# The first gather of a mixture of experts: its index from one comparison with the ranks of expert 0, and each token's 16 gates carried behind its row

## The reference

```python
g_logits = xt @ w_rg + b_rg                       # 4 groups
g_idx, g_p = argmax(g_logits), its softmax value
e_sel = (xt @ w_re + b_re)[group g_idx]           # the 4 experts of that group
top_v, top_i = top_k(e_sel, 2)
top_w = softmax(top_v) * g_p
gate[token, e] = top_w for the two chosen experts, 0 for the other 14
for e in range(16):
    h = silu(xt @ w_gate[e]) * (xt @ w_up[e])     # 1024 -> 512
    y += gate[:, e] * (h @ w_down[e])             # 512 -> 1024
x = layer_norm(alpha * x1 + y)
```

## Time and profile before

| | us |
|---|---|
| three runs | 896.71, 896.92, 899.1 |
| median | 896.92 |
| the profiled execution | 895.64 |
| its span | 894.0 |

### The profile page before, as it was taken

One profiled execution on the slowest core, in us unless ns is written; L12 is line 12 of the kernel. 1 busy time (PEld: TensorE's weight loads), 2 busy tenths in 40 slices (PEclk: granted clock), 3 DMA queues, 4 the chain that ended last, 5 costly groups with the idle time before them and its releaser, 6 DMA issues.

```text
span 894.0 us, 12720 instructions
## 1 busy us (share of the span) xinstructions
PE 820.6 (92%) x4267; PEld 713.6 (80%) x4268; DVE 590.3 (66%) x741; ACT 442.5 (50%) x495; POOL 272.6 (30%) x261
## 2 busy tenths in 40 slices
PE   6999999999999999279999999999999999999910
PEld 6999999998788886268888888888888888888810
DVE  4099999956676554889998983148911533947184
ACT  5211232546633223438888893258822734846252
POOL 1423564562000000034343432124312321433263
PEclk9999999999999999579999999999999999999965
DMA  8211111103647331569999999149962572983453
GB/s 291 55 48 47 47 47 48 47 1 114 242 176 271 118 124 48 154 231 313 392 392 370 394 394 324 29 101 364 390 218 63 160 229 46 350 306 65 110 241 139
DMA packets 59550, 167.57 MB, mean 187 GB/s; under 512 B 6841, under 2 KB 25274, under 8 KB 55430
## 3 DMA queue, kind: packets, MB, share of 16 engines
q1 hardware_dynamic: 51318, 144.57, 43.6%
q0 software_dynamic: 8208, 22.70, 11.6%
HBM read 144.79 MB, written 28.76 MB: 194 GB/s over the span
## 4 chain that ended last, share of the span: by engine, by line
PE 89%; DVE 6%; DMA 1%; issue 1%; ACT 1%; POOL 0%; POOLq 0%; SPq 0%; ACTq 0%; DVEq 0%
PE PS L1627 32%; PE PS L1378 19%; PE PS L1644 16%; PE PS L1557 10%; PE PS L1356 6%; PE PS L1528 2%; DVE C L1125 1%; PE PS L1405 1%; PE PS L1445 1%; PE PS L1509 1%; DVE RAW L1298 1%; DVE BIG L399 1%; DMA F<-in_x_prompt 1%; DMA F<-x_rows,MIX 0%; PE PS L1468 0%
## 5 line engine op out<-in xcount | busy, mean ns | idle before, releaser
L1627 PE MATMUL PS<-BIG,TH 128*128 128x512 f32 x1248 | 295.9, 393 | 1.5 <-DVE TH L1281 1.5
L1627 PEld LDWEIGHTS PS<-BIG,TH 128*128 128x128 f32 x1248 | 233.6, 189 | 49.4 <-issue 1.9
L1378 PE MATMUL PS<-BIG,WD 128*128 128x352 f32 x1080 | 177.4, 325 | 0.0
L1378 PEld LDWEIGHTS PS<-BIG,WD 128*128 128x128 f32 x1080 | 174.9, 188 | 0.9
L340 DVE TENSOR_TENSOR BIG<-RAW,BIG 128x2048 fp32r<-128x2048 f32 x64 | 145.1, 2288 | 24.1 <-ACT BIG L943 24.1
L1644 PE MATMUL PS<-WD,TH 128*128 128x512 f32 x624 | 155.8, 399 | 0.0
L1644 PEld LDWEIGHTS PS<-WD,TH 128*128 128x128 f32 x624 | 113.6, 189 | 22.1
L943 ACT ACTIVATE BIG<-RAW 128x2048 fp32r<-128x2048 f32 x64 | 119.3, 1908 | 15.6 <-PE PS L1557 7.9
L293 DVE SCALAR_TENSOR_TENSOR PS<-RAW,C,PS 128x512 f32<-128x512 f32 x174 | 115.4, 746 | 0.0
L1557 PE MATMUL PS<-BIG,WD 128*128 128x512 f32 (+1 forms) x432 | 100.7, 392 | 1.8 <-DVE BIG L399 1.8
L1557 PEld LDWEIGHTS PS<-BIG,WD 128*128 128x128 f32 (+1 forms) x432 | 76.7, 179 | 22.7 <-issue 1.3
(11 more groups left out here) (217 smaller groups left out, 770.1 us busy)
## 6 DMA issues: line engine op xcount, KB each, us to landing
RAW<-in_w_gate SPq DMA_DIRECT2D x64, 512.0 KB, 7.5
RAW<-in_w_up SPq DMA_DIRECT2D x64, 512.0 KB, 9.0
MIX<-in_w_down SPq DMA_DIRECT2D x32, 1024.0 KB, 10.5
F<-in_w_in SPq DMA_DIRECT2D x17, 512.0 KB, 4.1
F<-in_x_prompt SPq DMA_DIRECT2D x10, 512.0 KB, 4.8
x_rows<-F SPq DMA_DIRECT2D x9, 512.0 KB, 2.7
sum_rows<-F SPq DMA_DIRECT2D x9, 512.0 KB, 3.6
RAW<-in_w_out SPq DMA_DIRECT2D x4, 1024.0 KB, 6.1
```

The source lines that it names most:

```text
L1378: mm = pe.matmul(bank(3 * q + g, GRP), win[:, q, ws, c, :], xT[:, xs_, c, g * GRP:(g + 1) * GRP], start=(c == 0 and ws + xs_ == 0), stop=( ...
L1627: mm = pe.matmul(bank(h), xe[:, xs_, c, :], w, start=(c == 0 and xs_ + ws == 0), stop=(c == KD - 1 and xs_ == 1))
```

## The change

*A first index of its own.* VectorE compares, for the nine tiles of tokens, the rank in expert 0 (with 1,024 taken off for its members, `FAR`) with the numbers -1024 to -897. The result `ohf` is a one-hot of the place within the first tile, for the first 128 members of expert 0. Nine matmuls of two columns sum two parts of the token's number into bank 5, and `idxc` is made from them. The first gather waits for this, for the stored rows and for the stored gates, and no longer for the table.

*Gates behind the rows.* The gate weights are worked out ahead of the ranks, spread over 16 columns (`gate_rows`) and stored by SP into 16 new columns of `x1_dram`, whose rows are now 1,040 long. Each gather brings them along; GpSimd copies them (`keep_gates`) into 16 columns of `gates` for each tile, and `y_copy` takes the column of tile and expert. The one-hots `otw`, their eighteen matmuls and the sums behind them are gone.

*Order.* On TensorE the transposes of the first tile now stand ahead of the table's matmuls. On VectorE `xe_lo` of the first tile stands ahead of the table, and `lo_unit` 1 to 5 all behind the table.

```diff
-    x1_dram = nc.dram_tensor("x1_rows", (TOK + P, D), F32).ap()
+    x1_dram = nc.dram_tensor("x1_rows", (TOK + P, D + NE), F32).ap()
...
+        ohf = mx(NT * P // 2).bitcast(BF16).rearrange("p (i m) -> p i m", i=NT)
+        igf, key0, pm = mx(P), mx(NT), mx(1)
+        vc0 = mx(NT).bitcast(BF16).rearrange("p (i w) -> p i w", w=2)
+        firstf = mx(2)
...
+        gate_rows, gate_part = (mx(NT * NE).rearrange("p (i e) -> p i e", i=NT) for _ in range(2))
+        gates = mx(NE * NTAB)
...
+        xg_gated = F2[:, 0:D + NE]
...
                 for u in range(6):
                     wait_lo(sp, e - 1, u)
                     load_unit(sp, e, u)
+                    if u == 0 and isinstance(e, int):
+                        sp.wait_ge(S("gates_spread"), 1)
+                        sp.dma_start(x1_dram[0:SEQ, D:].rearrange("(i p) e -> p i e", p=P), gate_rows[:, 0:NT - 1, :]
+                                     ).then_inc(S("gates_stored"), 16)
+                        sp.dma_start(x1_dram[SEQ:TOK, D:], gate_rows[0:NS, NT - 1, :]).then_inc(S("gates_stored"), 16)
...
             def gather(t):
-                pool.wait_ge(S("index_copied"), t + 1)
+                pool.wait_ge(S("index_copied"), t)
+                pool.wait_ge(S("gates_in"), t)
                 pool.tensor_tensor(carrier[:, 0:1], epsc, epsc, ALU.add)
-                pool.indirect_dma_start(xg, None, x1_dram, bass.IndirectOffsetOnAxis(ap=idxc, axis=0),
+                gather_rows()
+
+            def gather_rows():
+                pool.indirect_dma_start(xg_gated, None, x1_dram, bass.IndirectOffsetOnAxis(ap=idxc, axis=0),
                                         bounds_check=TOK - 1, oob_is_err=False
                                         ).then_inc(S("rows_in"), 16)
 
+            def keep_gates(t):
+                pool.tensor_copy(gates[:, ds(t * NE, NE)], xg_gated[:, D:]).then_inc(S("gates_in"), 1)
+
+            pool.wait_ge(S("x1_stored"), 16 * NT)
+            pool.wait_ge(S("gates_stored"), 32)
+            pool.wait_ge(S("first_index"), 1)
+            gather_rows()
+            pool.wait_ge(S("rows_in"), 16)
+            keep_gates(0)
             pool.wait_ge(S("table_ready"), 1)
-            index(0)
-            pool.wait_ge(S("x1_stored"), 16 * NT)
-            gather(0)
-            pool.wait_ge(S("rows_in"), 16)
             index(1)
             pool.wait_ge(S("xe_turned"), 1)
             gather(1)
             pool.wait_ge(S("rows_in"), 32)
+            keep_gates(1)
             index(2)
...
-                act.wait_ge(S("gates_ready"), 1)
+                act.wait_ge(S("gates_in"), t + 1)
                 act.activation(yrow, PS[:, 5:7, :].rearrange("p b n -> p (b n)"), ACT.Copy,
-                               scale=gates[:, ds(t, 1)]).then_inc(S("y_copied"), 1)
...
-            dve.wait_ge(S("route_consts"), 6)
+            dve.wait_ge(S("route_consts"), 8)
+            dve.tensor_copy(vc0[:, :, 0], tokid[:, 0:NT]).then_inc(S("first_values"), 1)
...
+            dve.wait_ge(S("exps"), 2)
+            do(dve.tensor_reduce(gsum, ge, AX, ALU.add))
+            do(dve.reciprocal(gp, gsum))
+            do(dve.tensor_scalar(rs, ex, ALPHA, ALPHA, ALU.mult, ALU.add))
+            do(dve.reciprocal(rs, rs))
+            do(dve.tensor_tensor(wgt[:, 0], rs, gp, ALU.mult))
+            do(dve.tensor_tensor(wgt[:, 1], wgt[:, 0], ex, ALU.mult))
+            for k, out in enumerate((gate_rows, gate_part)):
+                do(dve.tensor_tensor(out, flat[k], over(wgt[:, k], NE), ALU.mult))
+            dve.tensor_tensor(gate_rows, gate_rows, gate_part, ALU.add).then_inc(S("gates_spread"), 1)
+
             dve.wait_ge(S("ranked"), 1)
+            rk = bank(7, NT * NE).rearrange("p (i e) -> p i e", i=NT)
+            do(dve.scalar_tensor_tensor(key0, Mb[:, :, 0], -float(FAR), rk[:, :, 0], ALU.mult, ALU.add))
+            dve.tensor_scalar(vc0[:, :, 1], key0, -1.0, pm, ALU.mult, ALU.add).then_inc(S("first_values"), 1)
+            dve.wait_ge(S("x1_ready"), NT)
+            dve.tensor_tensor(ohf, igf.rearrange("p (i m) -> p i m", i=1).to_broadcast((P, NT, P)),
+                              key0.rearrange("p (i m) -> p i m", m=1).to_broadcast((P, NT, P)), ALU.is_equal
+                              ).then_inc(S("first_hot"), 1)
             counts_ps = bank(7)[:, NT * NE:(NT + 1) * NE]
...
+            dve.wait_ge(S("first_sum"), 1)
+            do(dve.tensor_copy(firstf, bank(5, 2)))
+            dve.scalar_tensor_tensor(idxc, firstf[:, 0:1], padc, firstf[:, 1:2], ALU.add, ALU.add
+                                     ).then_inc(S("first_index"), 1)
...
-            dve.wait_ge(S("exps"), 2)
-            do(dve.tensor_reduce(gsum, ge, AX, ALU.add))
-            do(dve.reciprocal(gp, gsum))
-            do(dve.tensor_scalar(rs, ex, ALPHA, ALPHA, ALU.mult, ALU.add))
-            do(dve.reciprocal(rs, rs))
-            do(dve.tensor_tensor(wgt[:, 0], rs, gp, ALU.mult))
-            do(dve.tensor_tensor(wgt[:, 1], wgt[:, 0], ex, ALU.mult))
-            dve.wait_ge(S("table_sum"), 1)
-            do(dve.tensor_copy(tabf, bank(6, 2 * NTAB)))
-            dve.scalar_tensor_tensor(table, tabf[:, 0:NTAB], padc, tabf[:, NTAB:], ALU.add, ALU.add
-                                     ).then_inc(S("table_ready"), 1)
-
-            part = [wpart[0][:, 0], wpart[0][:, 1], wpart[1][:, 0]]
-            do(dve.tensor_copy(part[0], wgt))
-            do(dve.tensor_tensor(wrem[0], wgt, part[0], ALU.subtract))
-            do(dve.tensor_copy(part[1], wrem[0]))
-            do(dve.tensor_tensor(part[2], wrem[0], part[1], ALU.subtract))
-            for h in range(3):
-                dve.tensor_tensor(otw[:, :, :, h, :], ohe,
-                                  part[h].rearrange("p k (i m) -> p k i m", m=1).to_broadcast(four), ALU.mult
-                                  ).then_inc(S("gate_hot"), 1)
-
-            lo_unit(dve, 0, 1)
-            lo_unit(dve, 0, 2)
...
-            dve.wait_ge(S("gate_sum"), 1)
-            do(dve.tensor_copy(gatep, bank(7, 3 * NTAB)))
-            do(dve.tensor_tensor(gates, gatep[:, 2 * NTAB:], gatep[:, NTAB:2 * NTAB], ALU.add))
-            dve.tensor_tensor(gates, gates, gatep[:, 0:NTAB], ALU.add).then_inc(S("gates_ready"), 1)
+            dve.wait_ge(S("table_sum"), 1)
+            do(dve.tensor_copy(tabf, bank(6, 2 * NTAB)))
+            dve.scalar_tensor_tensor(table, tabf[:, 0:NTAB], padc, tabf[:, NTAB:], ALU.add, ALU.add
+                                     ).then_inc(S("table_ready"), 1)
             do(dve.tensor_scalar(tabf[:, 0:NTAB], tabf[:, 0:NTAB], padc, None, ALU.add))
             do(dve.tensor_tensor(tabf[:, 0:NTAB], tabf[:, 0:NTAB], tabf[:, NTAB:], ALU.add))
             do(dve.tensor_scalar(tabf[:, NTAB:], tabf[:, 0:NTAB], float(SEQ), 4096.0, ALU.is_lt, ALU.mult))
             dve.scalar_tensor_tensor(table_s, tabf[:, 0:NTAB], -float(SEQ), tabf[:, NTAB:], ALU.add, ALU.add
                                      ).then_inc(S("sample_table"), 1)
-            for u in (3, 4, 5):
+            for u in range(1, 6):
                 lo_unit(dve, 0, u)
...
+            pe.wait_ge(S("first_values"), 2)
+            pe.wait_ge(S("first_hot"), 1)
+            for i in range(NT):
+                M = rows_of(i)
+                mm = pe.matmul(bank(5, 2), ohf[0:M, i], vc0[0:M, i], start=(i == 0), stop=(i == NT - 1))
+            mm.then_inc(S("first_sum"), 1)
...
+            pe.wait_ge(S("rows_in"), 16)
+            for c in range(KD):
+                mm = turn(bank(2 + c // 4)[:, (c % 4) * P:(c % 4 + 1) * P], xg[:, c:D:KD], P)
+                if c == KD // 2 - 1:
+                    mm.then_inc(S("half_turned"), 1)
+            mm.then_inc(S("xe_turned"), 1)
             for c in range(2):
                 pe.wait_ge(S("one_hot"), c + 1)
                 for i in range(NT):
                     mm = pe.matmul(bank(6, 2 * NTAB), ohp[0:M, c, i], oht[0:M, c, i].rearrange("p h m -> p (h m)"),
                                    start=(c + i == 0), stop=(c == 1 and i == NT - 1))
             mm.then_inc(S("table_sum"), 1)
...
-            for c in range(2):
-                for i in range(NT):
-                    M = rows_of(i)
-                    if c + i == 0:
-                        pe.wait_ge(S("gate_hot"), 3)
-                    mm = pe.matmul(bank(7, 3 * NTAB), ohp[0:M, c, i], otw[0:M, c, i].rearrange("p h m -> p (h m)"),
-                                   start=(c + i == 0), stop=(c == 1 and i == NT - 1))
-            mm.then_inc(S("gate_sum"), 1)
-            pe.wait_ge(S("rows_in"), 16)
-            for c in range(KD):
-                mm = turn(bank(2 + c // 4)[:, (c % 4) * P:(c % 4 + 1) * P], xg[:, c:D:KD], P)
-                if c == KD // 2 - 1:
-                    mm.then_inc(S("half_turned"), 1)
-            mm.then_inc(S("xe_turned"), 1)
```

More of the change, by code:

```diff
@@ L50 @@
 EPS = 1e-5
+FAR = 1024
 ALPHA = 2.0 ** 0.25
@@ L727, in tile @@
                 pool.wait_ge(S("rows_in"), 16 * t + 48)
+                keep_gates(t + 2)
```

(7 more changed lines are left out.)

32 lines of the change are left out of this document (10 added, 22 removed).

## The result

| | before | changed |
|---|---|---|
| median us | 896.60 | 898.73 |
| lowest and highest of 12 | 895.58, 899.10 | 897.52, 901.36 |
| profiled execution, span | 895.64, 894.0 | 900.63, 899.0 |

The ratio is 1.0024, 95% interval 1.0014 to 1.0034: the changed kernel is 2.1 us slower, where 2.5 us faster was forecast. The time lies above the range.

What follows compares the result with a forecast made beforehand. Routing before the first tile was taken as the limit, TensorE being never idle afterwards. The tile starts 4.9 us sooner, subtractions take back 2.4: −2.5, profiled 893.1, median 894.4 us; range 892.9 to 898.0.

Steps and rivals of the forecast that it cites:

- What bounds the kernel: Expert stage: TensorE never idle, tiles repeat every 17.79 us, so a gain counts only if the first tile ends earlier.
- Routing and first index: Routing on VectorE and TensorE: gates spread at 370.2, the first gather's index ready at 373.6.
- The gate store: SP's store before the first gather: issued at 370.2, landing 1.0 behind a load of 374.4, at 375.4; bounds 373.6 and 377.4.
- late-store rival: Gate stores before the first gather land late: loss after 377.9; at 380.4 a loss of 2.5, 899.4 us; chance 0.14.
- The first tile: Tile 0: gather lands at 380.4, tile starts at 384.1, 4.9 sooner; waits for subtractions leave 2.5 at its first half's end.
- the bound: Best case at the first tile: store done at 373.6, so the index sets the gather's start; gain 3.6 us.
- The clock in the stuttering half: Tile 0's first half: TensorE's clock falls or isn't raised between waits for subtractions; only 1.0 won, 895.9 us; chance 0.14.
- The gain is absorbed: Expert 1's loads leave as subtractions end but are wanted 2.5 sooner; tile 1 waits, nothing is left, 896.9 us; chance 0.10.

Runs made afterwards that it cites:

- e16: Kernel before with half of the down weights left out of the loads of experts 1 to 15: 896.72 us, ratio 0.9996.
- e3: Changed kernel with the two gate stores issued ahead of expert 1's first loads: 894.49 us, ratio 0.9966.
- e9: Changed kernel with GpSimd's first store, 128 pieces of 4 bytes that nothing reads, cut to one piece: 893.70 us, ratio 0.9963.
- e1: Kernel before with only the subtractions of weight units 1 and 2 moved behind the table: 902.03 us, ratio 1.0048.
- e5: e3 with the subtraction of weight unit 1 moved right behind the first index: 896.38 us, ratio 0.9995.
- e14: e9 with the subtraction of weight unit 1 moved between the slots and the one-hots: 895.64 us, ratio 0.9980.
- e2: Changed kernel with the subtractions of weight units 1 and 2 moved back ahead of the split halves: 895.21 us, ratio 0.9974.
- e4: Changed kernel with the first gather reading acc_dram without waiting for the gates, and a second gather fetching that tile's gates: 897.14 us, ratio 1.0002.
- e11: e9 with the subtractions of weight units 1 and 2 given to GpSimd while VectorE routes: 901.72 us, ratio 1.0045.
- e12: e9 with the subtractions of weight units 1 and 2 moved back ahead of the split halves: 895.20 us, ratio 0.9977.
- e13: Kernel before with only GpSimd's first store cut to one piece: 896.82 us, ratio 1.0002.
- e8: e1 with half of the down weights left out of the loads of experts 1 to 15: 898.82 us, ratio 1.0020.
- e17: Changed kernel with half of the down weights left out of the loads of experts 1 to 15: 895.53 us, ratio 0.9981.
- e7: Changed kernel with the two gate stores issued on ScalarE's queue, the loads left first: 899.58 us, ratio 1.0030.

## Why the prediction was wrong

*What bounds the kernel* was read rightly as far as it went: the second tile's start decides. But "TensorE is never idle" in the loop was taken to mean that a tile which comes sooner stays sooner. In windows of 20 us the transfers of the kernel before ran at a share of 1.03 to 1.04, 374 to 393 GB/s, from 429 to 549, which the mean of 0.74 over the whole stage hides. (The share alone does not tell that limit: with half loads, e16, it was 0.96 to 1.02 there, at 323 to 349 GB/s and without a wait.) That a part of the stage has a second resource at its limit was not priced.

*Routing and first index.* Right: the sum of the gate arrays ended at 370.66 (370.2 forecast), the index at 373.8 (373.6).

*The gate store* is the step that failed first. "I take 1.0 behind it, 375.4" tied it to a load that was to land at 374.4 as before. It landed at 379.61 in the profiled execution, and by medians this lateness costs 4 to 5 us (e3 and e9 against the changed kernel). The late-store rival named the place, but not the reason: 64-byte pieces are not dear (2 us for 1,056 in e9); the loads ahead were stalled by 128 pieces of 4 bytes issued 8 us earlier. That rival's price comes close: a store at 379.6 makes a loss of 1.7, 898.6. That is luck, since the profiled execution lost 2.6 at the tile and 2.3 in a loop that the rival did not have. The rule that was weighed there, of "DMA: Bandwidth & Descriptors", Specifications, in the Trainium skill, on transfers under 512 B, was weighed for the wrong store: for the gate stores e9 speaks against a high price, for the 4-byte pieces e9 agrees with one, though what in the engines stalls is not shown. The profile of before had the mark: a load of 512 KB that took 12.6 us in a stretch whose transfers had a mean share of 0.43.

*The first tile.* With the store out of the way (e3) each step is there: gather at 375.92, landing at 380.0 (380.4 forecast, 380.5 by its own terms), tile at 384.19, waits for subtractions in the first half, ScalarE's first use of it at 393.16. The forecast 393.7 was 0.5 late, since the subtractions began 0.55 behind the tile's start and not 1.35. So 3.1 came where 2.5 was forecast (ScalarE's first use against 396.27), and with the index alone as the limit (e9) 3.5 where 3.6 was the bound. That e3's 894.49 is the forecast's 894.4 is luck again: more was won at the tile, and the loop took some of it back.

*The clock in the stuttering half* did not come where transposes, table and tile follow one another: it reached 1.00 at 390 in e3, as the argument from the earlier trace rows had it. In e1, with 1.50 us idle ahead of the tile and 0.66 within it, it came: 0.50 up to 397.

*The gain is absorbed* was given 0.10 and looked for in tile 1, where nothing waited. The other half of what failed lies here. That "all are wanted 2.5 sooner" was seen, but the lead of expert 1's loads over the second tile falls from 23.4 to 18.5 us with the new order, and with the transfers at their limit that is missed 100 to 120 us later, near 512 to 532. Order alone (e1) shows it best: 2.1 lost at the first tile, 2.8 in the loop. In the table ten of the kernels with all loads fall in two groups: stretches of 427.1 to 428.3 with a lead of some 23, of 429.0 to 431.0 with 18.5. But e5 and e14, which gave more of it to unit 1 alone (31.9 and 27.0), have 428.6 and 430.0. By the lead of unit 2's load instead all thirteen fall in two: at least 21.0 in the kernel before, e2, e4, e11, e12 and e13, with stretches up to 428.3; 16.2 to 17.7 in the others, with 428.6 and more. No run moved that load alone, and each stretch is of one execution. Shown is that lighter loads take the loss away, and that the loss is TensorE's wait for up weights; that the lead is the cause is argued.

*In sum*, by medians: the order loses 2.1 at the first tile and 2.8 in the loop (e8, e16, e1), the change without the order wins 2.0 (e2). That makes a loss of 2.9, where 2.1 was measured. e17 splits it otherwise, 1.2 won at the tile and 3.3 lost in the loop; the two splits differ by less than such differences are known to.

## What to carry to other kernels

A step moved behind the critical path still starts transfers: write down by how much each load's lead over its use shrinks, and look for the next stage where the transfers are at their limit, however far off. The wait for a small store was here a wait for what the transfer engines held just then, on either queue (e7); a load that lands late in an otherwise idle stretch is a warning to be explained before something is put behind it. And the tiny store that nothing reads was not free.

## What was not expected of the hardware

- 128 pieces of 4 bytes, issued at 362.7, held the loads at 29 GB/s in 369 to 370, where with one piece they moved 397; landings went from 7.6 and 9.1 us to 14.7 and 16.2.
- Stores on ScalarE's queue were nearly as late as on SP's (7.4 and 8.5 us). The Trainium skill, "DMA: Bandwidth & Descriptors", Queues, rings and completion order, says that a transfer's count comes only behind earlier writes of the same engine, across its queues; e7 agrees.
- A subtraction of 2,048 columns on GpSimd (4.5 us) held a VectorE instruction of 36 columns for 4.6 us (e11).
- A wait of 2.1 us in the loop cost 3.9: the granted clock was 0.95 and 0.96 in the two windows of 20 us around it (e9). Waits of 1.5 (e3) and 1.7 us (e14) left it at 1.00.
